# Seven block products instead of eight in a feed-forward product, with the conditioning sums moved to another stage

## What is computed

```python
h = layer_norm(x)
u_glu, z, xbc, dt_raw, gate_a, gate_b = split(h @ w_in)
y_a = conformer_branch(u_glu)              # depthwise convolution of 31 taps
y_b = ssd_branch(z, xbc, dt_raw)           # state-space scan; xbc has its own 4-tap convolution
mix = (sigmoid(gate_a) * y_a + sigmoid(gate_b) * y_b) @ w_o
h = layer_norm(alpha * h + mix)
ffn = conv_ffn(h, w_ffn_up, ffn_dw_w, ffn_dw_b, w_ffn_down)   # up, 3-tap convolution, silu gate, down
h = layer_norm(alpha * h + ffn)
```

```python
mod = silu(c) @ w_ada + b_ada              # 1024 -> 6144: the "conditioning sums"
sh1, sc1, g1, sh2, sc2, g2 = split(mod, 6)
h = rmsnorm(x) * (1 + sc1) + sh1
proj = h @ w_in2 ...
```

## Time and profile before

| | |
|---|---|
| time, median of 3 runs (lowest to highest) | 1336.68 us (1335.11 to 1338.78) |
| the profiled execution, its own time | 1338.18 us |
| its span | 1336.3 us |
| PE busy | 1302.5 us, 97% |
| DVE busy | 746.6 us, 56% |
| ACT, POOL busy | 275.9 us, 60.7 us |

### The profile page before, as it was taken

The page is one execution under the profiler, slowest core; times in us unless marked ns, Lnnn a source line. Parts: engine busy times, 40 slices in busy tenths (PEclk is TensorE's granted clock), DMA queues, the critical chain, the costliest instruction groups (busy, mean ns, idle before and its releaser), DMA issues.

```text
span 1336.3 us, 19717 instructions
## 1 busy us (share of the span) xinstructions
PE 1302.5 (97%) x7543; PEld 925.0 (69%) x7558; DVE 746.6 (56%) x1571; ACT 275.9 (21%) x582; POOL 60.7 (5%) x60
## 2 busy tenths in 40 slices
PE   8999999999999999999899999999999999999997
PEld 6888888888899888899694888854333433343332
DVE  4552389999436877787677786244332332332322
ACT  2311133220204000000343431124111211112112
POOL 0002113000000111100000000000000000000001
PEclk9999999999999999999999999999999999999999
DMA  7345233345557988946335148679999999999995
GB/s 271 128 145 170 93 123 124 125 156 176 179 182 256 328 285 317 315 118 232 127 127 189 64 166 339 252 270 366 403 427 427 426 429 427 427 427 428 425 422 219
DMA packets 123714, 351.02 MB, mean 263 GB/s; under 512 B 4848, under 2 KB 66544, under 8 KB 110320
## 3 DMA queue, kind: packets, MB, share of 16 engines
q1 hardware_dynamic: 122016, 348.68, 68.7%
q10 hardware_dynamic: 1616, 1.20, 0.3%
HBM read 348.82 MB, written 1.05 MB: 262 GB/s over the span
## 4 chain that ended last, share of the span: by engine, by line
PE 77%; DVE 10%; DMA 7%; issue 3%; ACT 2%; DVEq 1%; POOL 0%; POOLq 0%; SPq 0%; ACTq 0%
PE bank L902 34%; PE bank L1434 20%; DMA arena<-in_w_gate 7%; PE bank L954 6%; PE bank L1188 3%; PE bank L1402 3%; DVE arena L2126 2%; PE bank L1524 2%; PE bank L1250 2%; DVE scratch L2140 1%; PE bank L1150 1%; PE bank L974 1%; PE bank L1138 1%; DVE stat L2197 0%; DVEq L2126 0%
## 5 line engine op out<-in xcount | busy, mean ns | idle before, releaser
L902 PE MATMUL bank<-hT,dense 128*128 128x256 f32 x1792 | 390.5, 380 | 0.8 <-ACT hT L1625 0.8
L902 PEld LDWEIGHTS bank<-hT,dense 128*128 128x128 f32 x1792 | 339.3, 190 | 50.5 <-issue 4.9
L1434 PE MATMUL bank<-arena,scratch 128*64 128x512 f32 x768 | 189.3, 599 | 4.2 <-DMA arena<-in_w_gate 4.2
L902 PE MATMUL bank<-arena,dense 128*128 128x256 f32 x704 | 153.7, 380 | 0.4 <-DVE arena L2202 0.4
L902 PEld LDWEIGHTS bank<-arena,dense 128*128 128x128 f32 x704 | 133.3, 190 | 20.0 <-issue 2.0
L1434 PEld LDWEIGHTS bank<-arena,scratch 128*64 128x64 f32 x768 | 59.3, 138 | 103.0 <-issue 94.0
L1434 PE MATMUL bank<-arena,hT 128*64 128x512 f32 x416 | 113.4, 595 | 0.7 <-ACT hT L1912 0.7
L2126 DVE SCALAR_TENSOR_TENSOR arena<-arena,par 128x256 f32<-128x256 f32 x240 | 97.8, 489 | 0.0
L2758 DVE TENSOR_TENSOR scratch<-scratch,bank 128x512 f32<-128x512 f32 x64 | 41.2, 684 | 92.5 <-PE bank L1524 91.1
L1434 PEld LDWEIGHTS bank<-arena,hT 128*64 128x64 f32 x416 | 34.7, 137 | 62.3 <-issue 60.0
L2776 DVE SCALAR_TENSOR_TENSOR resid<-bank,lamp,resid 128x512 f32<-128x512 f32 x32 | 24.0, 751 | 94.1 <-PE bank L1434 94.1
(11 more groups left out here) (408 smaller groups left out, 1517.5 us busy)
## 6 DMA issues: line engine op xcount, KB each, us to landing
arena<-in_w_down SPq DMA_DIRECT2D x22, 2048.0 KB, 26.0
arena<-in_w_gate SPq DMA_DIRECT2D x21, 2048.0 KB, 23.9
dense<-in_w_in SPq DMA_DIRECT2D x17, 2048.0 KB, 8.1
arena<-in_w_up SPq DMA_DIRECT2D x15, 2048.0 KB, 23.2
arena<-in_w_ada SPq DMA_DIRECT2D x12, 2048.0 KB, 12.2
dense<-in_w_ffn_up SPq DMA_DIRECT2D x22, 1024.0 KB, 7.4
dense<-in_w_up SPq DMA_DIRECT2D x10, 2048.0 KB, 21.7
arena<-in_w_up SPq DMA_DIRECT2D x14, 1024.0 KB, 22.4
```

Source lines behind the costliest of these rows:

```text
L902: last = mm(dst, chunk(k, m), src[:, k, :], start=k == 0, stop=k == k_n - 1)
L1434: last = mm(dst[e * CAP:(e + 1) * CAP, :], tokens(k, e), w[e][k], start=k == 0, stop=k == k_n - 1)
```

## The change

It does five things.

1. Tiles 2 to 21 of `up` are made with seven block products (`fast_up`), in the same order of pieces as `qk` and with its corrections (`fix_first`, `fix_second`, `fix_third`, now shared). VectorE adds the blocks of weights once a unit, over 1024 columns (`up_weight_sums`, two instructions a tile), and the tokens' blocks once (`up_token_sums`).
2. `up` has four weight buffers.
3. The first of the three taps moves from VectorE to ScalarE (`first_taps`, two instructions a tile); VectorE keeps four.
4. The conditioning sums, their loads and the silu of `c` move to the first layer: after every second tile of `xbc` (groups 0 to 5) and of `glu` (6, 7), then 8 to 11 around `conv_out`. The loops of SyncE and VectorE over `up` are written out.
5. In the first tile of `down` the third product waits for the activations chunk by chunk, and semaphores are shared (`norm_out`, `norm_sq`, `norm_part`).

```diff
 def buffer(n):
+    if UP0 <= n < UP0 + UNIT["up"][1]:
+        return (0, 1, 4, 2)[(n - UP0) % 4]
...
-            stage("xbc", 6, flat, lambda u: wi[:, :, ds(u * 512 + C_XBC, 512)])
+            for u in range(6):
+                load("xbc", u, flat, wi[:, :, u * 512 + C_XBC:(u + 1) * 512 + C_XBC])
+                if u == 1:
+                    sp.dma_start(c_act, c_rows).then_inc(sem_("c_in"), 16)
+                    load_ada(0)
+                    load_ada(1)
+                elif u > 1:
+                    load_ada(u)
+            for u in range(4):
+                load("glu", u, halves, wglu2[:, :, :, u * 256:(u + 1) * 256])
+                if u < 3:
+                    load_ada(6 + u)
...
+            def fast_up(i, block):
+                t, u, j = i + 2, 1 + i // 2, i % 2
...
+                for n, p in enumerate(BLOCK[block]):
+                    for k in range(4):
...
+                        last = mm(b[:, SLOTS[p], :], left, right, start=k == 0, stop=k == 3)
+                last.then_inc(tile_done if block == "third" else sem_("fast_part"), 1)
+            for block, i in ORDER_UP:
+                fast_up(i, block)
...
-                product(first[:, 2, :], r1[:, DK:KF, :], hi[:, :, TOK[0]])
+                for k in range(DK):
+                    begin(sem_("act_ready"), DK + k + 1)
+                    mm(first[:, 2, :], r1[:, DK + k, :], hi[:, k, TOK[0]], start=k == 0, stop=k == DK - 1)
...
+            first_taps(0)
+            first_taps(1)
+            for i in range(NFAST_UP):
+                if i >= 3:
+                    first_taps(i - 1)
+                copy_up(i)
+                if i != 2:
+                    silu_gate(i - 1 if i >= 3 else i)
+            for t in (19, 20, 21):
+                first_taps(t)
                 silu_gate(t)
...
-            def xbc_tiles(i):
+            def xbc_tiles(i, first=False):
                 for t in range(4):
...
+                    if t % 2:
+                        if t == 1 and first:
+                            dve.wait_ge(sem_("x_std"), TT + 1)
+                        ada_sum(t // 2, i)
...
             for t in range(4):
                 glu(t)
+                if t % 2:
+                    ada_sum(6 + t // 2)
...
             open_gate("ssm_out", 3, 8)
+            ada_sum(8)
             for t in range(4):
                 open_gate("conv_out", t, 0)
...
+                if t in (0, 2, 3):
+                    ada_sum((9, None, 10, 11)[t])
...
+            up_weight_sums(1)
+            dve.wait_ge(sem_("norm_out"), GIVEN["n1"] + 2 * KD)
+            up_token_sums()
+            for i in range(NFAST_UP):
+                if i < 18:
+                    up_weight_sums(2 + i // 2, (2, 3) if i % 2 else (0, 1))
+                if i != 2:
+                    ffn_conv(i - 1 if i >= 3 else i)
+                fix_first("up", i)
+                if i:
+                    fix_second("up", i - 1)
+                if i >= 2:
+                    fix_third("up", i - 2)
+            fix_second("up", NFAST_UP - 1)
+            ffn_conv(19)
+            fix_third("up", NFAST_UP - 2)
+            act_sum(0)
+            fix_third("up", NFAST_UP - 1)
             ffn_conv(20)
-            act_sum(0)
             ffn_conv(21)
+            act_sum(1)
             down_weight_sums(1, (0,))
-            act_sum(1)
```

More of the change, by code:

```diff
@@ L131, with fast_order @@
 NFAST = 8
-def fast_order():
+def fast_order(tiles):
     out = [("first", 0)]
-    for t in range(NFAST):
-        if t + 1 < NFAST:
+    for t in range(tiles):
+        if t + 1 < tiles:
             out.append(("first", t + 1))
@@ L601, in _, with up @@
             down_arena(0, 1)
[L602 to L614, removed]
+            for u in range(2):
+                load("conv_out", u, flat, wco[:, :, u * 512:(u + 1) * 512])
+            load_ada(9)
+            load_ada(10)
+            load("mix", 0, flat, wo_[:, :, 0:512])
+            load_ada(11)
+            load("mix", 1, flat, wo_[:, :, 512:1024])
+            def up(u):
+                load("up", u, halves, wup2[:, :, :, u * 256:(u + 1) * 256])
             up(0)
@@ L1727, in _, with first_taps @@
-            f(c_act, c_act, ACT.Silu).then_inc(sem_("x_std"), 1)
-            def silu_gate(t, turn=0):
-                act.wait_ge(sem_("ffn_conv"), t + 1 + 4 * turn)
+            def first_taps(t):
+                if t < 2:
+                    b = wait_tile(act, "up", t)
+                else:
+                    b = bank[TILE["up", t] % NB]
+                    act.wait_ge(sem_("fast_fixed"), fast_count("up", "third", t - 2))
+                    act.wait_ge(sem_("act_ready"), t - 1)
+                for m in range(2):
+                    ch = t + m * KF
+                    f(half_t[:, t % 2, m * T:(m + 1) * T], b[:, m * T:(m + 1) * T], ACT.Identity,
+                      scale=par("ffn_w", ch * 3 + 2, 1), bias=par("ffn_b", ch, 1)).then_inc(sem_("first_taps"), 1)
@@ L1731, in silu_gate @@
+            def silu_gate(t):
+                act.wait_ge(sem_("ffn_conv"), t + 1)
                 if t >= 2:
-                    act.wait_ge(sem_("act_ready"), t - 1 + 4 * turn)
+                    act.wait_ge(sem_("act_ready"), t - 1)
                 f(sig_t[:, t % 2, :], half_t[:, t % 2, 0:T], ACT.Silu).then_inc(sem_("silu_gate"), 1)
-            for t in range(4):
-                silu_gate(t)
-            with act.Fori(0, 4) as i:
-                for t in range(4, 8):
-                    silu_gate(t, i)
@@ L2360, in _, with fast_places @@
-            dve.wait_ge(sem_("n1_out"), 2 * KD)
-            dve.wait_ge(sem_("x_std"), TT + 1)
-            ada_sum(0)
-            for t in range(4):
-                ffn_conv(t)
-                if t % 2:
-                    ada_sum(t // 2 + 1)
-            with dve.Fori(0, 4) as i:
-                own.turns(i, 24, 4)
-                for t in range(4, 8):
-                    ffn_conv(t, i)
-                    if t % 2:
-                        ada_sum(t // 2 + 1, i)
-            own.end()
+            def fast_places(name, t):
+                if name == "up":
+                    return v3(bank[TILE["up", t + 2] % NB][:], P), up_fixes[t % 3]
+                return v3(bank[TILE[name, t] % NB][:], P), fixes[t % 3]
@@ new lines, in fix_first, with fix_second @@
+            def fix_first(name, t):
+                b, f = fast_places(name, t)
+                dve.wait_ge(sem_("fast_copied"), copy_count(name, t))
+                tt(f[:, 3, :], f[:, 0, :], b[:, 2, :], ALU.add).then_inc(sem_("fast_fixed"), 1)
+                dve.wait_ge(sem_("fast_fixed"), fast_count(name, "first", t))
+                own.add(tt(f[:, 1, :], f[:, 3, :], f[:, 2, :], ALU.add))
+            def fix_second(name, t):
+                b, f = fast_places(name, t)
+                dve.wait_ge(sem_("fast_part"), part_count(name, "second", t))
+                own.wait()
+                tt(f[:, 3, :], f[:, 3, :], b[:, 2, :], ALU.add).then_inc(sem_("fast_fixed"), 1)
```

256 lines of the change are left out of this document (151 added, 105 removed).

## The result

| | before | after |
|---|---|---|
| time, median of 6 runs (lowest to highest) | 1336.31 us (1335.11 to 1338.78) | 1344.93 us (1342.78 to 1345.94) |
| the profiled execution, its own time | 1338.18 us | 1343.3 us |
| its span | 1336.3 us | 1341.4 us |
| PE busy, DVE busy | 1302.5, 746.6 us | 1293.9, 804.1 us |

The changed kernel is slower: ratio 1.0060, 95% interval 1.0048 to 1.0071. In the two traces TensorE is busy 8.6 us less, but the end is 5.1 us later: it stands (sits idle, waiting) 13.7 us longer, at several places of the first stage and at the end of `up`.

The account below looks back on a forecast made before the run. TensorE alone was taken to bound `up`, with the first stage's chain passing over VectorE at L2110. +15.1 (first stage) - 13.0 + 0.5 (`up`) + 3.2 + 1.0 (its end) = +6.8 us, so 1343.5 us; range 1334 to 1351.

Parts of the forecast that it names:

- `up`, TensorE: -13.0: In `up`: seven products a round take 6.26 us like `qk`, not 6.91, over twenty tiles: -13.0 us.
- +0.5 for VectorE: In `up`: VectorE's summed 6.32 us a tile is level with TensorE's 6.26, costing 0.5 us (0 to 1.5).
- rival 3: In `up`: collisions with GpSimd make VectorE the bound, 9 us more, 1352 us; chance 0.13.
- GpSimd and VectorE: In `up`: few collisions expected, as corrections read PSUM when GpSimd's product runs; one on every tile would lose 9 us.
- The first stage: +15.1: First stage: stand at the decays 7.4, group 7 4.7, clock 2.0 and 1.0; sum +15.1 us (10.6 to 17.4).
- With the loop's register work, up to 0.5 us a group: VectorE's `xbc` loop, first stage: register work adds up to 0.5 us to each group of sums.
- Loads "at nothing": First stage: late `xbc` and `glu` loads cost nothing, as up to 4 us hides in TensorE's stand at the decays.
- The end of `up`: +3.2: End of `up`: the last tile's longer path makes TensorE stand for VectorE's activation sum, then GpSimd; +3.2 us (2 to 4).
- Its clock, +1.0: End of `up`: a lower granted clock after the new idle stretch costs 1.0 us (0 to 2).
- Rival 1: Whole kernel: no lower clock and small end costs, -0.3 to +2 us, about 1338 us, no measurable change; chance 0.22.
- Rival 2: First stage: the sums hide if VectorE's loop takes 6 us less than summed; -4.6 us, 1332 us; chance 0.10.
- The prediction's price for one fall (2.0 us): Any new TensorE idle stretch of 2 us or more: the lower clock behind it may cost up to 2.0 us.

## Why the prediction was right, and where it was not

The forecast (1343.5 us, slower, the first stage over the gain of `up`) was the case that came: 1344.93 us. By its steps:

- **`up`, TensorE: -13.0, measured -12.6.** A round is 6.25 us, the pace of `qk`. The term "+0.5 for VectorE" was nearly nothing: one stand of 0.24 us. VectorE's round was summed to 6.32 us; with the first taps back it is 7.04 us, of which these take 508.30 - 507.27 = 1.03, so without them 6.0. The sum was 0.3 us too high: in that trace the five corrections take 1.73 us (503.15 to 504.88) where the earlier trace rows gave 1.90, the two weight additions 2.39 for 2.44 and the taps 1.90 for 1.98. Some 0.3 us more a round, from whatever cause, and VectorE would have bound `up`, so rival 3 was nearer than the result tells.
- **GpSimd and VectorE.** Of the 36 weight additions in the rounds two were longer than 1.22 us: 1.71 at 448.34 us and 1.42 at 454.05, each with GpSimd's product over it (448.25 and 453.66 us). From then on the product lies mostly over corrections that read PSUM (four of the five do), and they keep their 0.29 and 0.43 us, as the prediction said. By the rule of the Trainium skill that the prediction cites ("SBUF — State Buffer", section "Who interferes with whom"), an instruction of VectorE with two inputs in SBUF contends with one of GpSimd that reads SBUF, and with at most one input there it doesn't. The trace agrees: the two additions grew by 0.5 and 0.2 us, the corrections by nothing. GpSimd's product itself took 0.73 us here, not 1.28.
- **The first stage: +15.1, measured +15.35, by a sum whose parts were off both ways.** Group 1 cost 4.6, group 7 4.4 to 4.6, the clock 2.7 for 3.0. The stand of 7.4 us at the decays came as four stands, and only 3.37 us of it there. Two parts failed. "With the loop's register work, up to 0.5 us a group" did not come: the groups took 4.58 us in the loop as outside, and VectorE's loop was 1.7 us shorter than taken (57.53 to 117.49). And `wdt` was not looked at: I costed SyncE's queue and its waits, but the new loads, issued from 4 to 10 us, delay a transfer of ScalarE's queue that is issued behind them at 12.17 us and takes 15.9 us instead of 6.9, and tile 4 starts at 57.53 us, 2.1 later than I worked out. The two nearly cancel; that the term fits to 0.3 us is luck.
- **Loads "at nothing":** 1.37 and 0.36 us at 86 and 101 us, as sized, and hidden by the decays: with the load of `w_ada` later they are 1.41 and 0.67, and the gain is still the whole 2.3. When VectorE's loop is faster they go by themselves.
- **The end of `up`: +3.2, measured 2.7,** by the two engines named (VectorE's activation sum, then GpSimd). The sum had taken GpSimd's product at 1.28 us, from a row where it collides with VectorE; it took 0.73 here. Its clock, +1.0, did not come in the trace of after (22 records in 2.62 us behind the stand); in four other kernels with the same stand it did, see below.
- **Rival 1** (no lower clock) fell: the clock was at 0.50 behind both stands of the first stage, and holding it gains 2.7 us in the trace. **Rival 2** fell: the list of VectorE is in order, and the sums did not hide. But its condition, a loop 6 us shorter, is met when the loop is written out (the decays come 10 us earlier), which the prediction did not see as an edit within reach.
- **Between 5.5 us in the traces and 8.6 in the medians.** In the trace of after the clock did not fall behind the stands at `wdt` and at the end of `up`; in traces of its variants it did at the first in three of six and at the second in four of six, for 1.5 to 1.7 us. Before's own profiled execution lies 1.9 us over its median and after's 1.6 under. Which execution had which falls is not on record, but the mean granted clock of each is, and within a kernel it goes with the time: of the 11 executions with the loop written out the four shortest (1334.3 to 1335.0 us) had 0.994 to 0.995 and the four longest (1337.7 to 1339.9) 0.991 to 0.992; of after's six the two shortest had 0.992 and the others 0.989 to 0.991. So this part is likely the clock's, but not shown stand by stand.

## What to carry to other kernels

Work that is moved off an engine "with idle time" has to be placed by that engine's list, not by its average: the same twelve groups cost 15 us where they stood in front of reads that another engine waits for, and nothing once two of them stood a step away, the loop between them was shorter and one of their loads came later. A saving on the bounding engine holds only as long as the next one keeps pace; here 1.0 us a tile of VectorE decides over all 12.6. And when loads are added ahead of others, look at every queue that lands in the same stretch, not only the one they are issued on.

## What the runs showed of the hardware

Whether the granted clock falls behind a stand differs from one profile to the next, at equal stands. Behind the layer norm that follows `down` TensorE idles 1.90 to 1.91 us in every kernel; the same 16 records then take 5.41 us in five profiles (before, after, and three of the variants) and 3.72 in seven. After, and the kernel with group 7 earlier:

```profile
643.40 5.41 PE L1005 MATMUL bank<-scratch,con 128*128 128x256 f32 x16 [1.90 <-ACT scratch L1843]
```

```profile
639.07 3.72 PE L1005 MATMUL bank<-scratch,con 128*128 128x256 f32 x16 [1.91 <-ACT scratch L1843]
```

The stand for `wdt` (2.1 to 2.5 us) was followed by a unit of 14.08 us in four profiles and of 14.8 to 15.8 in four, and seven of these eight kernels are the same program up to there; the one of 1.95 us at the end of `up` by 22 records in 2.62 us in three and in 4.07 to 4.25 in four. The stand for the decays was followed by a fall in five profiles (3.18 to 3.37 us) and by none in the one with the second load later (3.00 us). The prediction's price for one fall (2.0 us) was near (1.5 to 1.7). The same stand had it in some profiles and not in others, and that fits spreads of 3 us and more within one kernel, which go with the granted clock (above). What decides it the runs don't show.

The other surprise is what a register loop costs on VectorE: four taps with waits on its own results took 2.57 us a half tile in the loop and 2.01 written out, for instructions of the same 0.48 us. In the loop VectorE is idle 0.18 to 0.3 us ahead of most of them; which part of the loop's register work that is, the runs don't separate.
